# Issuing the routed experts' down weights from ScalarE's DMA queue instead of SyncE's

## Chip, cores and metric

The kernel runs on one core of a Trainium2 chip. The metric is the device time of one execution in microseconds (us), as the median of several runs. Besides TensorE (PE, with its weight loads as PEld), VectorE (DVE), ScalarE (ACT), GpSimd (POOL) and SyncE (SP), the core has 16 DMA engines. They serve several queues: q1 holds what SyncE issues, q10 what ScalarE issues, q0 what GpSimd issues.

## What is computed

One layer of an encoder on 512 tokens of 1024 elements, all in float32: a token mixer (sparse attention beside a gated recurrence), then a mixture of experts. The change is in the second part. Of 64 experts each token uses 8, beside a shared one:

```python
def _moe(u, w_router, router_bias, w_gate, w_up, w_down, ws_gate, ws_up, ws_down):
    scores = jax.nn.sigmoid(t @ w_router)
    ...                                   # best 4 of 8 groups, then the best 8 experts
    gates = jnp.zeros((T, N_EXPERTS)).at[jnp.arange(T)[:, None], top_e].set(w)
    ...
        h = jax.nn.silu(jnp.einsum('td,edf->tef', xb, w_gate)) * jnp.einsum('td,edf->tef', xb, w_up)
        return jnp.einsum('tef,efd->td', h * gb[:, :, None], w_down)
    ...
    shared = (jax.nn.silu(t @ ws_gate) * (t @ ws_up)) @ ws_down
    return routed + shared
```

Gate and up weights of an expert are 1024 x 256, its down weights 256 x 1024: three transfers of 1 MB for each expert, with one row of 8 KB on each of 128 partitions.

## The kernel before

Each engine has its own instruction stream, written out by hand; semaphores order the streams. The mixer fills the first 430 us or so. In the expert part there are `n_steps` steps, here 64, one for each expert. A step takes the rows of the tokens that chose its expert (128 at most), gathers them from DRAM (`u2_rows`) into `xg`, turns them with the PE, multiplies by gate and up weights, applies SiLU and product, turns the result, multiplies by the down weights and stores the 128 result rows (`expert_rows`). The steps run in a hardware loop that is unrolled by `UNROLL = 4`, with the first and the last four written apart. The semaphores count four tiles of the shared expert first, hence the `VIRT = 4` in the counts.

Weights lie in `wx`, in four slots, and step n uses slot n mod 4. Each slot has a semaphore for gate and up (`gu_full`) and one for down (`w_full`).

Products of the down weights and of half of gate and up are made in three passes with a high and a low part: ScalarE writes `wd_hi` and `gu_hi` (L640, L647), VectorE the differences `wd_lo` and `gu_lo` (L914, L919). There is one `wd_hi` buffer, so it can be written for one step when the down product of the step before is through (`y2_done`).

The order in one step, by engine:

- PE (L850): indices of the step after next (`tokens_of`, L804), gate and up product (L756, L761), then the wait for `gathered` and the transposes of the next step's rows (`turn_rows`, L811), then the down product of the step before (L783), then the turn of `hs` (L769).
- GpSimd (L581): waits for the indices of the step after next and gathers its rows (L568).
- VectorE: the two halves of the result row of the step before (`yrow`, L1076, L1077), the next indices (L1046, L1048, L1041), `wd_lo` (L914), `hT_lo` (L933), the product after SiLU (L908), the rows' copies (L924, L927), `gu_lo` (L919).
- ScalarE (L693): after `y2_done` writes `wd_hi` and `hT_hi`, then SiLU of this step (L660), `xT_hi` (L651), and `gu_hi` of the next (L647).
- SyncE (L519): after `gu_done` it loads gate and up of the step four later, after `y2_done` the down weights of the same, and after `y2_left` and `y2_right` it issues the store (L513).

After the loop come the last four steps, and in parallel GpSimd gathers `expert_rows` back for each token, in 32 gathers (L597) that begin when all but the last four stores have landed. The PE adds them up (L877), and the last layer norm follows.

The functions that the change touches, and what they call:

Of the kernel before, what the change touches and what calls it, by code (L numbers as in the profile page):

```python
# [21 lines left out]
NE, ED, NG, TG, EK = 64, 256, 8, 4, 8  # L22
# [12 lines left out]
MAXPASS = NT  # L35
UNROLL = 4
# [30 lines left out]
def build(nc, x, c, w_ada, b_ada, w_in, kv_norm_g, w_uk, w_uv, rel_bias, hgrn_lb, gnorm_g, w_out,  # L67
# [17 lines left out]
    with ExitStack() as ctx:  # L85
# [3 lines left out]
        def sem(name):  # L89
            return ctx.enter_context(nc.semaphore(name))  # L90
# [300 lines left out]
        y2_done = sem("y2_done")  # L391
# [13 lines left out]
        w_full = [sem(f"w_full{i}") for i in range(UNROLL)]  # L405
# [44 lines left out]
        wd_v = w_down[0].rearrange("e (p j) n -> e p (j n)", j=KF)  # L450
# [12 lines left out]
        def flat_weights(s):  # L463
            w = wx[:, s, :, :].rearrange("p a n -> p (a n)")
            return w[:, 0:2048], w[:, 2048:4096], w[:, 4096:6144]

        def steps(eng):

            eng.wait_ge(route_ready, 1)
            more = eng.value_load(nit[0:1, 0:1], min_val=0, max_val=(MAXPASS - 1) * NE)  # L470
            return eng.snap(more + NE)

        def sync_tail(sp):
            sp.wait_ge(rows_used, ROWS)
            for dst, src in zip(flat_weights(SHARED), (ws_gate[0], ws_up[0], ws_down[0])):
                j = KD if src.shape[0] == D else KF
                sp.dma_start(dst, src.rearrange("(p j) n -> p (j n)", j=j)).then_inc(shared_loaded, 16)

            def load(s, e, parts=range(3)):
                for k in parts:  # L480
                    dst, src = flat_weights(s)[k], (wg_v, wu_v, wd_v)[k]
                    sp.dma_start(dst, src[e] if isinstance(e, int) else src[bass.ds(e, 1)].rearrange("o p n -> (o p) n"))\
                        .then_inc(w_full[s] if k == 2 else gu_full[s], 16)

            for t in range(NT):
                if t == NT - 1:
                    sp.wait_ge(wo_done, NT)
                    load(0, 0)
                sp.wait_ge(u2_ready, t + 1)
                sp.dma_start(u2_d[t * P:(t + 1) * P, :], u2[:, t % 2, :]).then_inc(u2_stored[t % 2], 16)  # L490
            sp.wait_ge(x1_ready, NT)
            sp.wait_ge(xg_zero, 2)
            for b_ in range(4):
                sp.dma_start(y_d[T * EK - (b_ + 1) * P:T * EK - b_ * P, :], xg[:, b_ % 2, :]).then_inc(ends_zeroed, 16)
            load(2, 2, (0, 1))
            load(3, 3, (1, 2))
            sp.wait_ge(gu_done, VIRT)
            sp.wait_ge(ends_zeroed, 64)
            for b_ in range(2):
                sp.wait_ge(gathered[b_], 16)  # L500
            load(1, 1, (0, 1))
            load(2, 2, (2,))
            load(3, 3, (0,))
            sp.wait_ge(y2_done, VIRT)
            load(1, 1, (2,))
            n_steps = steps(sp)

            def store(u, row, waits, stored):

                sp.wait_ge(y_stored, stored)  # L510
                sp.wait_ge(y2_left, waits)
                sp.wait_ge(y2_right, waits)
                sp.dma_start(y_d[bass.ds(row, P), :], yb_[:, u % 2, :]).then_inc(y_stored, 16)  # L513

            def first_row(col):
                return sp.value_load(base_i[0:1, bass.ds(col, 1)], min_val=0, max_val=T * EK)

            n16 = sp.snap(n_steps * 16)
            with sp.Fori(0, n_steps - UNROLL, UNROLL) as i:  # L519
                i16 = sp.snap(i * 16)  # L520
                for u in range(UNROLL):
                    done = sp.snap(i + (VIRT + u + 1))
                    stored = sp.snap(i16 + (u + 4) * 16)
                    row = first_row(i + u)
                    e = sp.snap((i + (UNROLL + u)) % NE)

                    sp.wait_ge(gu_done, done)
                    load(u, e, (0, 1))
                    sp.wait_ge(y2_done, done)
                    load(u, e, (2,))  # L530
                    store(u, row, done, stored)
            for u in range(UNROLL):
                done = sp.snap(n_steps + (VIRT + u + 1 - UNROLL))
                row = first_row(n_steps + (u - UNROLL))
                stored = n16 + u * 16

                done = sp.snap(sp.to_reg(done), min_val=1, max_val=1024)
                store(u, row, done, stored)
            sp.dma_start(lnrow[:, 0, :], ln2_g[0:1, :].broadcast_to([P, D])).then_inc(ln_loaded, 16)
            sp.dma_start(lnrow[:, 1, :], ln2_b[0:1, :].broadcast_to([P, D])).then_inc(ln_loaded, 16)  # L540
            for t in range(NT):
                if t < NT - 1:
                    sp.wait_ge(row_out, t + 1)
                else:
                    sp.wait_ge(last_out, 1)
                sp.dma_start(out_t[:, t, :], x1[:, t, :]).then_inc(out_stored, 16)
            sp.wait_ge(out_stored, 16 * NT)
# [90 lines left out]
        def act_tail(act):  # L638
            def weights_high(s):
                act.activation(wd_hi[:], flat_weights(s)[2], ACT.Copy).then_inc(wd_hi_ready, 1)  # L640

            def gate_up_high(s, loaded, used):

                act.wait_ge(gu_full[s], loaded)
                if used is not None:
                    act.wait_ge(gu_done, used)
                act.activation(gu_hi[:], gate_up_weights(s)[:, :, 0:J3, :], ACT.Copy).then_inc(gu_hi_ready, 1)  # L647

            def rows_high(n):
                act.wait_ge(xt2_done, n + 1)  # L650
                act.activation(xT_hi[:], ps[2][:, 0:J3 * P].rearrange("p (j n) -> p j n", n=P), ACT.Copy).then_inc(xt2_act, 1)  # L651
# [4 lines left out]
            def silu_gate(n, u):  # L656
                act.wait_ge(gu_done, n + 1)
                if not isinstance(n, int) or n >= 2:
                    act.wait_ge(ht_done, n - 1)
                act.activation(hs[:, u % 2, :], ps[u % 2][:, 0:ED], ACT.Silu).then_inc(silu_ready, 1)  # L660

            def turned(n, u):
                act.wait_ge(ht_done, n + 1)
                if not isinstance(n, int) or n >= 2:
                    act.wait_ge(y2_done, n - 1)
                act.activation(hT_hi[:, u % 2, :, :], ps[4][:, 0:ED].rearrange("p (j n) -> p j n", n=P),
                               ACT.Copy).then_inc(ht_ready, 1)
# [22 lines left out]
            shared_out(3)  # L690
            n_steps = steps(act)

            def expert(i, u, more=True):  # L693
                first = isinstance(i, int)
                if not first or u >= 1:
                    act.wait_ge(y2_done, i + (VIRT + u - 1))
                    act.wait_ge(w_full[(u - 1) % UNROLL], 4 * i + (16 if u >= 1 else 0))
                    weights_high((u - 1) % UNROLL)
                    turned(i + (VIRT + u - 1), u - 1)
                silu_gate(i + (VIRT + u), u)  # L700
                if more:
                    rows_high(i + (u + 1))
                    gate_up_high((u + 1) % UNROLL, 8 * i + (32 if u < UNROLL - 1 else 64), i + (VIRT + u + 1))

            for u in range(UNROLL):
                expert(0, u)
            with act.Fori(UNROLL, n_steps - UNROLL, UNROLL) as i:
                for u in range(UNROLL):
                    expert(i, u)
            tail = act.snap(act.to_reg(n_steps - UNROLL), min_val=NE - UNROLL, max_val=MAXPASS * NE)  # L710
            for u in range(UNROLL):
                expert(tail, u, u < UNROLL - 1)

            def diagonals(first, end):
                for d in range(first, end):
# [460 lines left out]
        def _(sp):  # L1176
# [50 lines left out]
            load_rows(7)  # L1227

            sync_tail(sp)

        @block.gpsimd
# [30 lines left out]
        def _(act):  # L1262
# [215 lines left out]
            act.wait_ge(u2_ready, NT)  # L1478
            act.activation(wd_hi[:], flat_weights(SHARED)[2], ACT.Copy).then_inc(wd_hi_ready, 1)  # L1479
            act_tail(act)  # L1480

        @block.tensor
# [618 lines left out]
```

## Time and profile before

| | |
|---|---|
| runs | 1210.47, 1210.78, 1211.69 us, median 1210.78 |
| the profiled execution | 1211.71 us, span from first to last instruction 1209.9 us |
| busy over the span | PE 93%, PEld 63%, DVE 77%, ACT 40%, POOL 19% |
| bytes | 335.68 MB, of these q1 293.15 MB, q10 8.53 MB, q0 33.58 MB |
| share of 16 DMA engines | q1 64.3%, q10 2.0%, q0 7.5% |

The span lies 1.8 us below the time of the same execution, and that execution is 0.9 us above the median. The shares are means over the whole kernel. The expert loop, from 500 to 1120 us, is the longest stage, and has to be read in its own windows. Matmuls are pipelined, so a busy PE is not a PE at its peak, but a PE without any idle time is one that waits for nobody.

### The profile page before, as it was taken

Reading aid. Unit: us, or ns where it says so; the run is one execution under the profiler, and the core shown is the slowest. Engines: PE = TensorE matmul, PEld = TensorE weight load, DVE = VectorE, ACT = ScalarE, POOL = GpSimd, SP = SyncE. Lnnn points to the kernel's source line nnn. Section 1 sums busy time; section 2 is a strip of 40 time slices with the busy share of each in tenths; the row PEclk is TensorE's granted clock in tenths of the full one; section 3 lists DMA queues with packets and bytes.
Section 4 is the critical chain, followed back from the end, with each engine's and each line's share of the span. In section 5 each row is a group of like instructions: output and inputs, shape, how many; then the busy total and the mean of one; then the engine's idle time right before and its main releaser. Section 6 shows DMA issues by size and latency. Waiting matters only on the chain.

```text
span 1209.9 us, 14757 instructions
## 1 busy us (share of the span) xinstructions
PE 1131.0 (93%) x4784; PEld 760.1 (63%) x4786; DVE 935.9 (77%) x1388; ACT 481.2 (40%) x619; POOL 229.7 (19%) x119
## 2 busy tenths in 40 slices
PE   2699999997999999999999999999999999999965
PEld 2353446885654477677777777777777777777632
DVE  3578997976443777898888888888888888888857
ACT  0214324336651021444444444444444444444411
POOL 0000000000000000122222222222222222222670
PEclk9799999998999989999999999999999999999988
DMA  9992421109302063799999999999999999999793
GB/s 348 356 398 91 50 32 70 70 3 333 118 1 105 35 271 114 277 357 392 382 387 384 384 383 382 374 385 371 392 382 379 376 381 382 376 393 389 259 406 132
DMA packets 77817, 335.68 MB, mean 277 GB/s; under 512 B 14376, under 2 KB 16296, under 8 KB 52824
## 3 DMA queue, kind: packets, MB, share of 16 engines
q1 hardware_dynamic: 58680, 293.15, 64.3%
q0 software_dynamic: 13824, 33.58, 7.5%
q10 hardware_dynamic: 5280, 8.53, 2.0%
q8 instruction: 19, 0.31, 0.1%
q14 instruction: 14, 0.11, 0.0%
HBM read 309.51 MB, written 42.48 MB: 291 GB/s over the span
## 4 chain that ended last, share of the span: by engine, by line
PE 88%; DVE 4%; DMA 3%; ACT 2%; issue 2%; POOL 1%; ACTq 0%; SPq 0%; DVEq 0%; POOLq 0%
PE ps L756 18%; PE ps L783 15%; PE ps L761 14%; PE ps L1521 8%; PE ps L811 5%; PE ps L1751 5%; PE ps L1529 3%; PE ps L821 2%; PE ps L1592 2%; DMA ring<-in_w_ada 2%; PE ps L877 2%; PE ps L1615 2%; PE ps L1605 2%; PE ps L1721 2%; PE ps L1549 1%
## 5 line engine op out<-in xcount | busy, mean ns | idle before, releaser
L568 POOL DMA_INDIRECT xg<-u_rows,idx x64 | 182.9, 2858 | 496.8 <-DVE idx L1048 496.5
L756 PE MATMUL ps<-wx,xT 128*128 128x512 f32 x512 | 235.4, 602 | 0.1
L919 DVE TENSOR_TENSOR gu_lo<-wx,gu_hi 128x2048 fp32r<-128x2048 f32 x64 | 146.6, 2291 | 56.9 <-ACT gu_hi L647 56.9
L914 DVE TENSOR_TENSOR wd_lo<-wx,wd_hi 128x2048 fp32r<-128x2048 f32 x65 | 148.5, 2284 | 2.8 <-ACT wd_hi L1479 2.2
L756 PEld LDWEIGHTS ps<-wx,xT 128*128 128x128 f32 x512 | 92.1, 190 | 92.0 <-issue 91.8
L660 ACT ACTIVATE hs<-ps 128x256 f32<-128x256 f32 x68 | 26.0, 383 | 302.0 <-PE ps L761 281.3
L640 ACT ACTIVATE wd_hi<-wx 128x2048 fp32r<-128x2048 f32 x64 | 122.4, 1913 | 26.3 <-PE ps L783 26.3
L761 PE MATMUL ps<-gu_hi,xT_hi 128*128 128x512 f32 x256 | 126.3, 493 | 0.5 <-DVE gu_lo L919 0.5
L647 ACT ACTIVATE gu_hi<-wx 128x2048 fp32r<-128x2048 f32 x64 | 122.1, 1908 | 0.0
L783 PE MATMUL ps<-wd_hi,hT_hi 128*128 128x512 f32 x272 | 112.7, 414 | 4.3 <-DVE hT_lo L933 4.3
L783 PE MATMUL ps<-wd_hi,hT_lo 128*128 128x512 f32 x272 | 107.3, 395 | 0.0
L783 PE MATMUL ps<-wd_lo,hT_hi 128*128 128x512 f32 x272 | 106.5, 391 | 0.0
L761 PE MATMUL ps<-gu_hi,xT_lo 128*128 128x512 f32 x256 | 101.2, 395 | 0.0
L761 PE MATMUL ps<-gu_lo,xT_hi 128*128 128x512 f32 x256 | 99.5, 389 | 0.0
L1521 PE MATMUL ps<-uT,ring 128*128 128x512 f32 x208 | 91.0, 600 | 0.0
L1521 PEld LDWEIGHTS ps<-uT,ring 128*128 128x128 f32 x208 | 39.9, 193 | 49.9 <-issue 48.8
L811 PEld LDWEIGHTS ps<-ident,xg 128*128 128x128 f32 x512 | 67.0, 191 | 5.2
L811 PE MATMUL ps<-ident,xg 128*128 128x128 f32 x512 | 67.2, 274 | 0.0
L761 PEld LDWEIGHTS ps<-gu_hi,xT_hi 128*128 128x128 f32 x256 | 48.2, 188 | 24.0 <-issue 16.3
L761 PEld LDWEIGHTS ps<-gu_lo,xT_hi 128*128 128x128 f32 x256 | 48.3, 188 | 23.6 <-issue 15.1
L551 POOL MEMSET tri<- 128x64 f32 x1 | 0.2, 151 | 331.3 <-PE ps L1761 331.3
L783 PEld LDWEIGHTS ps<-wd_hi,hT_hi 128*128 128x128 f32 x272 | 51.5, 189 | 14.0 <-DVE hT_lo L933 4.9
(317 smaller groups left out, 1869.6 us busy)
## 6 DMA issues: line engine op xcount, KB each, us to landing
wx<-in_w_gate SPq DMA_DIRECT2D x64, 1024.0 KB, 7.6
wx<-in_w_up SPq DMA_DIRECT2D x64, 1024.0 KB, 10.7
wx<-in_w_down SPq DMA_DIRECT2D x64, 1024.0 KB, 8.5
expert_rows<-yrow SPq DMA_DIRECT2D x64, 512.0 KB
ring<-in_w_ada SPq DMA_DIRECT2D x7, 2048.0 KB, 19.8
ring<-in_w_in SPq DMA_DIRECT2D x6, 2048.0 KB, 15.9
vg<-in_w_ada SPq DMA_DIRECT2D x2, 2048.0 KB, 13.3
fk<-in_w_ada SPq DMA_DIRECT2D x2, 2048.0 KB, 15.2
```

Of the source, the lines that this page charges most:

```text
L568: pool.indirect_dma_start(out=xg[:, buf, :], out_offset=None, in_=u2_d[:, :], in_offset=bass.IndirectOffsetOnAxis(ap=idx[:, col:col + 1], ...
L640: act.activation(wd_hi[:], flat_weights(s)[2], ACT.Copy).then_inc(wd_hi_ready, 1)
L647: act.activation(gu_hi[:], gate_up_weights(s)[:, :, 0:J3, :], ACT.Copy).then_inc(gu_hi_ready, 1)
L756: pe.matmul(bank, xT_raw[:, j - J3, :], raw[:, :, j, :], start=(j == J3), stop=False)
L761: mm = pe.matmul(bank, a[:, j, :], w[:, :, j, :], start=False, stop=(j == J3 - 1 and k == 2))
L783: mm = pe.matmul(ps[6 + half][:], a[:, u % 2, j, :], w[:, j, half * 512:half * 512 + 512], start=(k == 0), stop=(k == len(passes) - 1))
L811: mm = pe.transpose(ps[2 + k][:, j * P:(j + 1) * P], xg[:, buf, 4 * k + j::KD], ident[:])
L914: dve.tensor_tensor(wd_lo[s][:], w, wd_hi[:].bitcast(F32), ALU.subtract).then_inc(wd_ready, 1)
L919: dve.tensor_tensor(gu_lo[s][:, :, 0:J3, :], gate_up_weights(s)[:, :, 0:J3, :], gu_hi[:].bitcast(F32), ALU.subtract).then_inc(gu_lo_ready, 1)
L1521: mm = pe.matmul(bank[:], ring[:, SLOT[unit], j, col:col + P], uT[:, j, :], start=(j == 0), stop=(j == KD - 1))
L1529: mm = pe.matmul(bank[:, 0:w], uT[:, j, t * P:(t + 1) * P], ring[:, SLOT[unit], j, col:col + w], start=(j == 0), stop=(j == KD - 1))
L1751: mm = pe.matmul(ps[2 * (t % 2) + half][:], src[:, j % 4, t * P:(t + 1) * P], ring[:, SLOT[OUT0 + half], j, :], start=(j == 0), stop=(j == ...
```

## The change

SyncE no longer waits for `y2_done` in the loop and no longer issues the down weights there. ScalarE does: in each step from the third on it stops at `y2_done`, computes the address and issues the load of the down weights of the expert two after its own step, into the slot whose down product has just ended. The condition, the slot, the semaphore and the number of loads are those of before; the loads ahead of the loop stay with SyncE. In the last four steps it issues only in the first two. A bound in `tail` is narrowed for the address computation.

```diff
--- before.py
+++ after.py
@@ -526,8 +526,6 @@
 
                     sp.wait_ge(gu_done, done)
                     load(u, e, (0, 1))
-                    sp.wait_ge(y2_done, done)
-                    load(u, e, (2,))
                     store(u, row, done, stored)
@@ -690,10 +688,17 @@
-            def expert(i, u, more=True):
+            def next_down(i, u):
+                e = i + u + 2 if isinstance(i, int) else act.snap((i + (u + 2)) % NE)
+                src = wd_v[e] if isinstance(e, int) else wd_v[bass.ds(e, 1)].rearrange("o p n -> (o p) n")
+                act.dma_start(flat_weights((u + 2) % UNROLL)[2], src).then_inc(w_full[(u + 2) % UNROLL], 16)
+
+            def expert(i, u, more=True, ending=False):
                 first = isinstance(i, int)
                 if not first or u >= 1:
                     act.wait_ge(y2_done, i + (VIRT + u - 1))
+                    if (not first or u >= 2) and (not ending or u < UNROLL - 2):
+                        next_down(i, u)
                     act.wait_ge(w_full[(u - 1) % UNROLL], 4 * i + (16 if u >= 1 else 0))
                     weights_high((u - 1) % UNROLL)
                     turned(i + (VIRT + u - 1), u - 1)
@@ -707,9 +712,9 @@
-            tail = act.snap(act.to_reg(n_steps - UNROLL), min_val=NE - UNROLL, max_val=MAXPASS * NE)
+            tail = act.snap(act.to_reg(n_steps - UNROLL), min_val=NE - UNROLL, max_val=MAXPASS * NE - UNROLL)
             for u in range(UNROLL):
-                expert(tail, u, u < UNROLL - 1)
+                expert(tail, u, u < UNROLL - 1, True)
```

SyncE, one step inside the loop, before (with what each row waits for; ISA and REGISTER_ALU are register work):

```order
L482 ISA [waits gu_done]
L482 DMA wx<-in_w_gate 128x2048
L482 DMA wx<-in_w_up 128x2048
L482 DMA wx<-in_w_down 128x2048 [waits y2_done]
L510 REGISTER_ALU
L513 ISA [waits y2_right,y2_left,y_stored]
L513 DMA expert_rows<-yrow 128x1024
```

and after:

```order
L482 ISA [waits gu_done]
L482 DMA wx<-in_w_gate 128x2048
L482 DMA wx<-in_w_up 128x2048
L510 REGISTER_ALU
L513 ISA [waits y2_right,y2_left,y_stored]
L513 DMA expert_rows<-yrow 128x1024
```

The down load with its wait is gone, and the rest stands in the same order.

ScalarE, the second of the four steps in the loop, before:

```order
L697 REGISTER_ALU [waits y2_done]
L640 ACTIVATE wd_hi<-wx 128x2048 [waits w_full0]
L666 ACTIVATE hT_hi<-ps 128x256 [waits y2_done,ht_done]
L657 REGISTER_ALU
L660 ACTIVATE hs<-ps 128x256 [waits ht_done,gu_done]
L651 ACTIVATE xT_hi<-ps 128x512 [waits xt2_done]
L647 ACTIVATE gu_hi<-wx 128x2048 [waits gu_done,gu_full2]
```

and after:

```order
L694 ISA [waits y2_done]
L694 DMA wx<-in_w_down 128x2048
L702 REGISTER_ALU
L638 ACTIVATE wd_hi<-wx 128x2048 [waits w_full0]
L664 ACTIVATE hT_hi<-ps 128x256 [waits y2_done,ht_done]
L655 REGISTER_ALU
L658 ACTIVATE hs<-ps 128x256 [waits ht_done,gu_done]
L649 ACTIVATE xT_hi<-ps 128x512 [waits xt2_done]
L645 ACTIVATE gu_hi<-wx 128x2048 [waits gu_done,gu_full3]
```

Register work and the load stand between the wait for `y2_done` and `wd_hi`. The other activations keep their places.

## Rows read from the trace of the kernel before

**Rows 1.** Windows: stretch and length, busy us (instructions) by engine, PEclk, DMA share, GB/s

```profile
core 0: us, PE busy (x) PEld busy (x) DVE busy (x) ACT busy (x) POOL busy (x), PEclk, DMA share, GB/s
800.00:880.00 80.00, 80.00 (x365) 57.70 (x364) 67.47 (x88) 37.79 (x39) 23.69 (x8) 1.00 0.98 384
```

**Rows 2.** Timeline, 801 to 816 us: start, duration, engine (q: its sequencer), line, operation

```profile
801.77 2.94 POOL L568 DMA_INDIRECT xg<-u_rows,idx  x1 [7.33 <-DVE idx L1048]
...
807.85 0.33 SPq L482 DMA_DIRECT2D wx<-in_w_down  x1
807.85 1.91 ACT L640 ACTIVATE wd_hi<-wx 128x2048 fp32r<-128x2048 f32 x1 [0.36 <-PE ps L783]
...
809.67 0.37 ACT L666 ACTIVATE hT_hi<-ps 128x256 fp32r<-128x256 f32 x1
...
811.26 0.35 SPq L513 DMA_DIRECT2D expert_rows<-yrow  x1
...
811.83 2.29 DVE L914 TENSOR_TENSOR wd_lo<-wx,wd_hi 128x2048 fp32r<-128x2048 f32 x1
...
812.04 2.94 POOL L568 DMA_INDIRECT xg<-u_rows,idx  x1 [7.33 <-DVE idx L1048]
...
814.05 1.09 PEld L811 LDWEIGHTS ps<-ident,xg 128*128 128x128 f32 x8
...
814.48 0.38 ACT L660 ACTIVATE hs<-ps 128x256 f32<-128x256 f32 x1 [4.44 <-PE ps L761]
...
815.05 0.19 PEld L783 LDWEIGHTS ps<-wd_hi,hT_hi 128*128 128x128 f32 x1
```

**Rows 3.** DMA issues of the page: out<-in, queue, count, KB each, median us to landing

```profile
wx<-in_w_up SPq DMA_DIRECT2D x64, 1024.0 KB, 10.7
```

**Rows 4.** DMA issues in windows of one gather each; the last number is its landing

```profile
xg<-u_rows,idx POOLq DMA_INDIRECT x1, 10.6
...
xg<-u_rows,idx POOLq DMA_INDIRECT x1, 11.3
...
xg<-u_rows,idx POOLq DMA_INDIRECT x1, 11.4
...
xg<-u_rows,idx POOLq DMA_INDIRECT x1, 11.5
...
xg<-u_rows,idx POOLq DMA_INDIRECT x1, 11.7
...
xg<-u_rows,idx POOLq DMA_INDIRECT x1, 12.1
```

**Rows 5.** Line 568, all gathers of the expert loop

```profile
DMA to landing us min/median/max: 4.5/10.8/12.1
```

**Rows 6.** Timeline, issues by ScalarE: start, duration

```profile
17.44 0.55 ACTq L1266 DMA_DIRECT2D wuv<-in_w_uv  x1
18.01 9.69 ACTq L1266 DMA_DIRECT2D rbias<-in_router_bias  x1
...
278.48 0.38 ACTq L1387 DMA_DIRECT2D big<-bias_by_position  x1
```

**Rows 7.** DMA queues from 24 to 27 us: packets, MB, share of 16 engines

```profile
q1 hardware_dynamic: 260, 1.01, 87.1%
q10 hardware_dynamic: 262, 0.15, 16.7%
```

**Rows 8.** DMA queues from 282.25, 818.00, 822.25 (0.25 us each) and 812 (1 us)

```profile
q10 hardware_dynamic: 16, 0.03, 35.8%
...
q0 software_dynamic: 2, 0.01, 8.0%
...
q0 software_dynamic: 1, 0.00, 0.2%
...
q1 hardware_dynamic: 56, 0.43, 102.5%
```

**Rows 9.** Timeline, the end of the expert loop

```profile
1119.48 42.94 SPq L513 DMA_DIRECT2D expert_rows<-yrow  x5
...
1127.86 1.32 POOL L597 DMA_INDIRECT wx<-expert_rows,slot8i  x1 [5.30 <-DMA expert_rows<-yrow]
```

## The prediction

> **What bounds the kernel now.** I read the windows of the expert loop first. In a stretch of 80 us TensorE is busy for all 80.00 us at a granted clock of 1.00, VectorE for 67.5 and ScalarE for 37.8 us, and the 16 DMA engines for 0.98 of the time [rows 1]. Two things are full at once, TensorE and the DMA engines, and only the timeline tells which one sets the pace. One step lasts 10.27 us (the gathers of two steps start at 801.77 and 812.04), and TensorE has no idle time in it [rows 1, 2]. So TensorE sets the pace, and a change of queues can gain nothing inside the loop. The question is only whose slack it eats. I looked at three.
>
> Weights: each of the four slots is loaded anew as soon as its step is through, and wanted again some three steps, 30 us, later. The slowest of the loads, up, lands in 10.7 us in the median [rows 3]. None is near a wait.
>
> ScalarE: wd_hi starts at 807.85, hT_hi follows, and then ScalarE is idle for 4.44 us. VectorE takes up wd_hi only at 811.83 [rows 2].
>
> Row gathers: GpSimd starts one at 801.77, and the transposes that read its rows start at 814.05 [rows 2], 12.28 us later. The median of the 64 landings is 10.8 us and the longest 12.1 [rows 4, 5]. This is the only tight wait of the loop: 1.5 us in the median, 0.2 us once. It also hangs on how the DMA engines share their time, which is what the change alters. The order of the queues is therefore the argument, not their bytes.
>
> **What the change does, part by part.** It removes from SyncE one wait for y2_done and one issue per step (0.33 us at 807.85 [rows 2]). SyncE then stands at the wait for y2_left, y2_right and y_stored as before. The store still starts at 811.26, when VectorE has written the row, and the next gate and up loads follow it. They keep their start, so this part is worth 0.
>
> It adds to ScalarE one address computation, one issue and an earlier stop of its sequencer at y2_done. ScalarE's issues took 0.38 and 0.55 us where its queue had room [rows 6]. With the register work I take 0.5 us per step. Queued behind are wd_hi, hT_hi and the SiLU of the next step. Now wd_hi ends at about 809.8 (807.85 + 1.91) and would end at 810.3, 1.5 us before VectorE starts line 914 at 811.83. hT_hi would be ready at 810.5, and the 4.44 us of idle time before the SiLU take up the rest [rows 2]. Cost 0; if ScalarE lost over 1.5 us more, wd_lo would be late, and behind it the down product at 815.05.
>
> Bounding the issue itself: the longest one of ScalarE took 9.69 us [rows 6]. That was the seventh transfer in a row in its queue. Here each down load is alone in its queue and lands before the next is issued, so I take the short end.
>
> It moves 1 MB per step from SyncE's queue (q1) to ScalarE's (q10). The bytes and the total backlog of the DMA engines stay. What changes is whose turn it is. Where q1 and q10 both have work, they send packet for packet: 260 against 262 from 24 to 27 us [rows 7]. A gather (q0) that now trades turns with q1 alone would have two others between its packets, for as long as q10 is active.
>
> When is q10 active? A ScalarE issue at 278.48, while q1 was full, shows no q10 packet in the quarter of a microsecond from 282.00 and its first 16 in the one from 282.25: 3.8 us [rows 6, 8]. The gather's own instruction (812.04, 2.94 us long) ends at 814.98 and its first two packets stand in 818.00 to 818.25, 3.1 us later [rows 2, 8]. Counted from the gather's start, y2_done comes at 6.1 us (807.85 against 801.77) and ScalarE would issue at 6.2. So q10's packets begin at 9.3 to 10.0, and I take 9.7, between the two. The gather's packets run from 6.1 us to 0.3 us before it lands: the one that lands after 10.6 has its last packet in 822.25 to 822.50, at 10.2 to 10.4 [rows 4, 8]. **So the overlap is the last 0.6 us of a median gather, and up to 2.1 us of the slowest.** After that q10 has the next 5 us (8 packets on each engine, each beside one of q1) and is empty before the next gather's first packet.
>
> The price of a turn: in 812 to 813 us q1 alone sent 56 packets with 0.43 MB, in 102.5% of 16 engine-microseconds [rows 8]. That is about 52 packets of 8 KB at 0.31 us. A round of the gather now costs 0.31 us plus its own packet. The gather's packets are 4 KB rows (half of 0.31, some 0.16 us) or almost nothing. One q10 packet more therefore stretches it by 0.66 to 0.97 of its remaining time; I take 0.85. With landing L a gather would land at L + 0.85 (L - 0.3 - 9.7), and TensorE would wait for 1.85 L - 20.8 us where that is positive, from L = 11.24 on.
>
> Of the 28 landings that the trace tells between 540 and 1110 us (it tells every other one), three are 11.4, two 11.5, and one each 11.3, 11.7 and 12.1; the other 20 are 11.2 or less [rows 4] (a row that comes again stands once). The waits are 0.1 + 3 x 0.3 + 2 x 0.5 + 0.85 + 1.6 = 4.45 us, and doubled for the untold half 8.9 us. A wait gives something back: in the step in which TensorE waits, y2_done and the down load come later too, and the next gather has more time. Where the next gather would be late as well (8 in 28) this removes its wait; 8.9 less 8/28 of it is 6.4 us. Bounds: a start at 9.3 and a factor of 0.97 give waits from 10.96 on, some 21 us before and 12 to 15 after the same reduction; a start at 10.0 and 0.66 give 2.7 us before and 2 after.
>
> **The tail.** Behind the last down load stands the store of step 59, issued at 1119.48. GpSimd then waits 5.30 us, until 1127.86, for that store, before it begins the 32 gathers of expert rows [rows 9]. With the down load out of its queue the store could land earlier by at most that load's 8 packets per engine, 8 x 0.31 = 2.5 us. Against it: the engine that is last has the same packets to send in either order, and taking turns brings store and load to an end together. I take -0.9 us, between 0 and -2.5 and nearer to 0.
>
> **The sum.** 6.4 - 0.9 = +5.5 us. The profiled execution took 1211.71 us, of which 1209.9 are its span, and the median of the runs is 1210.78. The difference goes on the median: 1216.3 us, +0.45%.
>
> **What a page says.** The rows show the queues taking turns by packets [rows 7]. The Trainium skill, "DMA: Bandwidth & Descriptors", section "Queues, rings and completion order", says that each DMA engine goes round its queues packet by packet. The same page, section "Issuing engines are not separate DMA queues", says that issuing from several engines saves only the issuing sequencer's time. By the second rule the sum would be 0, by the first a third queue costs a waiting gather turns. Both can hold, since the bytes per second stay and one transfer's share falls; no run so far shows three queues at work.
>
> **Rivals.**
> No effect (0.36): the q10 packets start at 10.2 us or later, or the last engine's gather packets are already through. For it: the median gather has only 0.6 us of overlap, and 20 of 28 stay under the break-even of 11.24. Against it: eight do not. It gives 1210.8 less some of the tail, 1209.5 to 1212. This is also what the rule of the second section above comes to.
> Faster by the tail (0.13): the store of step 59 lands 2.5 us earlier, GpSimd's 32 gathers start as much earlier, and all behind them too, since TensorE has waits for just these gathers. It decides if the last engine sends the store before the load's last packets. 1210.8 - 2.5 = 1208.3.
> More than the overlap (0.05): ScalarE's issue blocks as in the 9.69 us row, or a third queue also puts off the gather's first packet. 1 us in each of 56 steps less 0.2 to 1.5 us of slack gives 1230 and more.
> The overlap as computed: 0.46, of which the lowest tenth lies within 0.2%.
>
> **How the numbers follow.** 0.2%, 2.4 us, is about what a measurement of this kernel can tell from no change. Slower by more: 0.41 + 0.05 = 0.46. Within: 0.36 plus 0.05 of the overlap's low end = 0.41. Faster: 0.13. The likeliest case gives 1216.3, on its own 1212.5 to 1226. The range takes in the tail's gain and the overlap's upper bound, and leaves out the fourth case: 1208.4 to 1226.
>
> **What would show it.** Each step right: TensorE idle before line 811, only in steps whose gather lands after 12.28 us; q10 packets first seen 9.3 to 10 us after a gather's start; the longest landings grow and the short ones do not; down loads land at 7 to 9 us, gate and up loads as before; ScalarE's idle before the SiLU falls from 4.44 to about 3.9 us. It is wrong if no gather lands after 12.28 us (then the second case), if VectorE waits for wd_hi inside the loop, or if GpSimd's 5.30 us shrinks to under 4 us and the loop keeps 10.27 us (then the third).

## The result and the profile after

The changed kernel takes 1222.80 us in the median of 13 runs (1214.31 to 1231.53). The kernel before, run beside it, takes 1213.37 (1210.37 to 1219.34, 13 runs). The ratio is 1.0075 [1.0055, 1.0096]: slower by about 9 us. The profiled execution took 1224.19 us, of which 1222.4 are its span, against 1211.71 and 1209.9 before: the span is 12.5 us longer. No ratio here counts one execution of 1488.74 us at a granted clock of 0.745, of the kernel under "The load behind the gather", which ran in a slower state of the core.

Parts 4 to 6 of the page of the kernel after (shares of the chain of waits; costliest groups with busy, mean ns and idle time before; DMA issues with their landing):

```profile
PE 70%; DMA 15%; DVE 5%; issue 4%; ACT 3%; POOL 2%; ACTq 0%; SPq 0%; POOLq 0%; DVEq 0%
...
L816 PEld LDWEIGHTS ps<-ident,xg 128*128 128x128 f32 x512 | 65.9, 192 | 18.7 <-DMA xg<-u_rows,idx 14.7
...
wx<-in_w_up SPq DMA_DIRECT2D x64, 1024.0 KB, 12.7
```

Line 4 of the page before:

```profile
PE 88%; DVE 4%; DMA 3%; ACT 2%; issue 2%; POOL 1%; ACTq 0%; SPq 0%; DVEq 0%; POOLq 0%
```

TensorE held 88% of the chain and now holds 70%; DMA went from 3% to 15%. The line that got a wait is 816, the row transposes (line 811 before): TensorE's weight loads wait 14.7 us in sum in front of them for the gathered rows. The up load lands 2.0 us later than in [rows 3], which nobody notices, since it has 30 us.

A window of 550 us, nearly the whole expert loop, in the columns of [rows 1], before and then after:

```profile
560.00:1110.00 550.00, 550.00 (x2461) 392.17 (x2460) 465.89 (x590) 266.37 (x268) 156.91 (x54) 1.00 0.99 383
```

```profile
560.00:1110.00 550.00, 542.74 (x2415) 383.59 (x2413) 456.84 (x578) 261.88 (x263) 153.73 (x52) 1.00 0.98 375
```

TensorE was busy for all of the 550 us. Now it stands idle for 7.3 of them, at the same granted clock of 1.00. It is waiting, not slower. These 7.3 us are less than the loop lost (below). PE's own waits for the gathered rows are shorter than those of its weight loads, 0.66 us against 1.08 in the step shown below and 8.5 against 14.7 in sum, and the 14.7 come nearer to the loss.

The time is located by one line of the trace, that of the 64 row gathers: the first and the last start bound the loop. Before:

```profile
L568 POOL DMA_INDIRECT xg<-u_rows,idx x64: 988/2939/3042, 463.6 to 1120.3; - x64
```

After, with those that waited for the rows (us, times) and the landings:

```profile
L566 POOL DMA_INDIRECT xg<-u_rows,idx x64: 985/2935/3042, 462.4 to 1131.4; - x64
...
  PEld ps L816: 14.7, 15
...
DMA to landing us min/median/max: 4.2/11.6/14.5
```

From first to last gather it was 656.7 us and is 669.0. The difference of the two spans, 12.5 us, splits into -1.2 ahead of the loop, **+12.3 in it** and +1.4 behind it. Landings were 4.5/10.8/12.1 [rows 5]; the median is 0.8 and the longest 2.4 us later, and the shortest is not. (The trace of the kernel before tells the landing of every other gather, so the median in [rows 5] is one of 32 and not of 64; this one tells all 64. The packets of q0 are there for every gather: counted over the 54 gathers 7 to 60, the last packet ends 10.6 us after the gather's start in the median before, and 11.3 us after the change. It ends later than 11.98 us, 0.3 us ahead of the 12.28, in none before and in 15 after, as many as there are waits.)

One such step on the timeline of the kernel after (815 to 830 us):

```profile
816.67 2.94 POOL L566 DMA_INDIRECT xg<-u_rows,idx  x1 [8.09 <-DVE idx L1053]
...
822.92 0.34 ACTq L694 DMA_DIRECT2D wx<-in_w_down  x1
...
823.40 1.91 ACT L638 ACTIVATE wd_hi<-wx 128x2048 fp32r<-128x2048 f32 x1 [1.01 <-PE ps L788]
...
826.81 2.29 DVE L919 TENSOR_TENSOR wd_lo<-wx,wd_hi 128x2048 fp32r<-128x2048 f32 x1
...
829.36 0.38 ACT L658 ACTIVATE hs<-ps 128x256 f32<-128x256 f32 x1 [3.78 <-PE ps L766]
...
829.98 0.97 PEld L816 LDWEIGHTS ps<-ident,xg 128*128 128x128 f32 x8 [1.08 <-DMA xg<-u_rows,idx]
```

Its gather and its landing in the list of DMA issues, and the first quarter of a microsecond (824.50 to 824.75) with packets of q10, ScalarE's queue:

```profile
xg<-u_rows,idx POOLq DMA_INDIRECT x1, 13.3
```

```profile
q10 hardware_dynamic: 2, 0.02, 75.5%
```

The gather starts at 816.67 and lands 13.3 us later, 1.0 us past the 12.28 us that it has, and TensorE waits 1.08 us. ScalarE issued the down load 6.25 us after the gather's start. Its packets begin 1.6 to 1.8 us after that, 7.8 to 8.1 us after the gather's start, when the gather has five microseconds to go. This step is a typical one: over the 54 the first q10 packet comes 8.3 us after the gather's start in the median, between 7.5 and 9.6. ScalarE itself loses nothing: wd_hi starts 1.01 us after its release instead of 0.36 [rows 2], ends at 825.31, and VectorE takes it up at 826.81, 1.5 us later.

### The profile page after: what moved, and what is told of

It reads as the page before. It is cut to its first block, busy times and chain, and to the rows that moved or that the text cites. A ratio compares the mean times of both kernels' runs of the same rounds, so it can differ in the third digit from the quotient of the medians.

```text
span 1222.4 us, 14787 instructions
## 1 busy us (share of the span) xinstructions
PE 1135.9 (93%) x4786; PEld 759.9 (62%) x4786; DVE 935.9 (77%) x1388; ACT 481.1 (39%) x619; POOL 230.5 (19%) x119
## 4 chain that ended last, share of the span: by engine, by line
PE 70%; DMA 15%; DVE 5%; issue 4%; ACT 3%; POOL 2%; ACTq 0%; SPq 0%; POOLq 0%; DVEq 0%
DMA xg<-u_rows,idx 12%; PE ps L761 12%; PE ps L788 10%; PE ps L766 9%; PE ps L1526 7%; PE ps L1756 4%; PE ps L816 4%; PE ps L1534 3%; PE ps L826 2%; PE ps L1597 2%; DMA ring<-in_w_ada 2%; PE ps L882 2%; PE ps L1620 2%; PE ps L1610 2%; PE ps L1726 2%
## 5 line engine op out<-in xcount | busy, mean ns | idle before, releaser
L924 DVE TENSOR_TENSOR gu_lo<-wx,gu_hi 128x2048 fp32r<-128x2048 f32 x64 | 146.6, 2291 | 56.9 <-ACT gu_hi L645 56.9
L816 PEld LDWEIGHTS ps<-ident,xg 128*128 128x128 f32 x512 | 65.9, 192 | 18.7 <-DMA xg<-u_rows,idx 14.7
## 6 DMA issues: line engine op xcount, KB each, us to landing
wx<-in_w_up SPq DMA_DIRECT2D x64, 1024.0 KB, 12.7
vg<-in_w_ada SPq DMA_DIRECT2D x2, 2048.0 KB, 13.1
```

The costliest lines, as they stand in the source:

```text
L816: mm = pe.transpose(ps[2 + k][:, j * P:(j + 1) * P], xg[:, buf, 4 * k + j::KD], ident[:])
L924: dve.tensor_tensor(gu_lo[s][:, :, 0:J3, :], gate_up_weights(s)[:, :, 0:J3, :], gu_hi[:].bitcast(F32), ALU.subtract).then_inc(gu_lo_ready, 1)
```

## The experiments

**The theory of turns:** a third active queue stretches the gather that it overlaps, and the price is the length of its turns in the gather's last microseconds. Rivals: ScalarE's stop and address work delay wd_hi; the bytes or the backlog matter and not the order; the difference is one of run to run. In the expectations a loop of "595.9 us" is counted from the sixth gather; the loop here is always counted from the first, which makes it 656.7 for the same kernel. Differences are the same either way.

**Once more, both.** The kernel before and the kernel after, unchanged, in a later comparison.

> The kernel before once more, for a second trace. If its spread of 1208.8 to 1222.8 us comes from outside the expert loop, the stretch from the fourth to the last row gather is 595.9 us again, whatever the total is. If it comes from late gathers in some executions, that stretch is longer where the total is above 1211 us, and TensorE waits before the row transposes.

> The changed kernel once more, for a second trace and a ratio beside the other two. Turn theory: waits of 8 to 20 us before the row transposes, the loop's stretch 604 to 616 us against 595.9, median landing 11.3 to 12, ratio 1.005 to 1.010. If the first trace was a chance: a loop near 596 us and a ratio below 1.003.

The kernel before: 1218.56 us in one profiled execution. The kernel after: 1.0092 [1.0065, 1.0119]. Line of the gathers, before again and then after again:

```profile
L568 POOL DMA_INDIRECT xg<-u_rows,idx x64: 985/2939/3043, 470.3 to 1127.0; - x64
...
  PEld ps L811: 0.2, 1
```

```profile
L566 POOL DMA_INDIRECT xg<-u_rows,idx x64: 987/2941/3044, 468.8 to 1131.0; - x64
...
  PEld ps L816: 6.7, 8
...
DMA to landing us min/median/max: 5.2/10.9/13.9
```

The loop of the kernel before is 656.7 us again, to a tenth, with one wait of 0.2. That of the kernel after is 662.2: +5.5, where the other trace had +12.3. The sum of the waits is a matter of how many gathers land beyond 12.28 us, 8 here and 15 there. The median landing is 10.9 us here, only 0.1 later than in [rows 5], but that is again every other gather; by the last packets of the 54 it is 10.9 against 10.3 in the kernel before again, 0.6 us later. The kernel before again took 6.8 us more than the first trace of it, nearly all ahead of the loop (first gather at 470.3, not 463.6). The first 120 us, first trace of before and then the second:

```profile
0.00:120.00 120.00, 87.16 (x284) 47.23 (x285) 74.88 (x112) 25.20 (x51) 3.77 (x16) 0.90 0.82 300
```

```profile
0.00:120.00 120.00, 87.56 (x269) 47.90 (x270) 69.55 (x94) 22.71 (x47) 3.77 (x16) 0.83 0.81 299
```

The granted clock was 0.90 and 0.83 (the third number from the end), and 269 products instead of 284 were through. It is so in all thirteen traces: in the four with a clock of 0.82 or 0.83 there the first gather starts at 468.5 to 470.9 us, in the nine with 0.90 to 0.93 at 460.6 to 466.3. This goes a long way to explain why single times of one kernel spread over 9 us. I therefore set the length of the loop, which is free of it, beside each ratio.

**ScalarE's share alone.** The kernel before, and ScalarE does all that the change gives it, but loads 8 bytes per partition into a buffer that nobody reads; SyncE still loads the down weights.

```diff
+            def next_down(i, u):
+                e = i + u + 2 if isinstance(i, int) else act.snap((i + (u + 2)) % NE)
...
+                act.dma_start(small_dst[:], src[:, 0:2]).then_inc(small_sem, 16)
```

> The kernel before, with its down loads left in SyncE's queue; ScalarE issues in the same place a load of 8 bytes per partition that nobody reads, with the same address work. Turn theory (a gather lands late because packets of 8 KB of a third queue come between its own): a turn of 8 bytes costs nothing, so gathers land after 10.8 us in the median as before, TensorE does not wait before its row transposes, ratio to before 0.998 to 1.002. Rival, ScalarE's time (the stop at y2_done, the register work and the issue cost the loop): the ratio is that of the changed kernel, 1.0075. Rival, bandwidth (q1 and q10 together move less per second): ratio 1.000 too, since hardly any bytes are on q10.

1.0009 [0.9986, 1.0031]. Its gathers, then its ScalarE on the timeline:

```profile
L570 POOL DMA_INDIRECT xg<-u_rows,idx x64: 984/2939/3043, 463.6 to 1121.0; - x64
...
  PEld ps L823: 1.0, 2
```

```profile
809.18 1.91 ACT L642 ACTIVATE wd_hi<-wx 128x2048 fp32r<-128x2048 f32 x1 [0.98 <-PE ps L795]
```

The same delay of wd_hi as in the kernel after (0.98 against 1.01 us), and a loop of 657.4, +0.7. ScalarE's work is not the cause. (This kernel waits besides for its own small load of the step before, which has long landed. Its q10 packets come later than those of the kernel after, 9.7 us after the gather's start in the median, so that it tests ScalarE's work and not the place of the packets.)

**The same load, later on ScalarE.** The kernel after with `next_down` moved behind `turned`, and in another run behind `silu_gate`:

```diff
-                    if (not first or u >= 2) and (not ending or u < UNROLL - 2):
-                        next_down(i, u)
                     act.wait_ge(w_full[(u - 1) % UNROLL], 4 * i + (16 if u >= 1 else 0))
                     weights_high((u - 1) % UNROLL)
                     turned(i + (VIRT + u - 1), u - 1)
+                    if (not first or u >= 2) and (not ending or u < UNROLL - 2):
+                        next_down(i, u)
                 silu_gate(i + (VIRT + u), u)
```

> The changed kernel, with ScalarE's issue of the down load moved behind wd_hi and hT_hi of the same step, some 2.3 us later; bytes and queues as in the changed kernel. Turn theory: q10's first packets fall 9.5 us or more after the gather's start instead of 7.5 to 9.5, when most gathers are through, and they are gone before the next gather's first packet at 16.4; waits before the row transposes fall from 14.7 us to under 3 us, ratio to before 1.000 to 1.002. ScalarE's time: the issue still stands in the stream, with less behind it, so 1.003 to 1.0075. Bandwidth: nothing changes, 1.0075.

1.0044 [1.0020, 1.0069]. Its timeline:

```profile
803.17 1.91 ACT L638 ACTIVATE wd_hi<-wx 128x2048 fp32r<-128x2048 f32 x1 [0.36 <-PE ps L788]
803.57 0.34 ACTq L694 DMA_DIRECT2D wx<-in_w_down  x1
```

The edit did not do what I meant: the issue stands behind two activations in the code, but ScalarE's sequencer issued it 0.40 us after the first of them had begun, while that one ran on. It came 6.48 us after the gather's start (797.09), 0.2 us later than in the kernel after, and the loop, from 466.3 to 1126.4, is 660.1 (+3.4). This run tells little of the place.

> The changed kernel, with the issue moved further, behind the SiLU of the step, some 13 us after the gather's start. Turn theory: q10's packets now run from about 15 to 20 us and meet the next gather's packets (16.4 to 20.8) from the first on; landings of 12.5 us and more in the median, TensorE waits in most steps, 0.5 to 1 us in the mean step, ratio 1.02 to 1.04. ScalarE's time: the issue stands in idle time and costs nothing, ratio 1.000. Bandwidth: 1.0075.

1.0422 [1.0391, 1.0452], 1263.11 us. The start of its loop's line and the waits:

```profile
L566 POOL DMA_INDIRECT xg<-u_rows,idx x64: 988/2939/3043, 460.6 to 1168.6; - x64
...
  PEld ps L816: 52.3, 34
```

Three of its gathers and the issue on the timeline:

```profile
790.61 2.94 POOL L566 DMA_INDIRECT xg<-u_rows,idx  x1 [7.98 <-DVE idx L1053]
802.61 3.02 POOL L566 DMA_INDIRECT xg<-u_rows,idx  x1 [9.07 <-DVE idx L1053]
812.87 2.94 POOL L566 DMA_INDIRECT xg<-u_rows,idx  x1 [7.23 <-DVE idx L1053]
```

```profile
805.19 0.34 ACTq L694 DMA_DIRECT2D wx<-in_w_down  x1
```

The same bytes in the same queue, issued 2.6 us after the start of a gather, so that they overlap all of it (the first q10 packet comes 6.4 us after the gather's start in the median, its own first at 6.5): the loop is 708.0, +51.3, with 52.3 us of waits. A step of 12.00 us is followed by one of 10.26 here, since a wait in one step gives the next gather more time. The place of the load in relation to the gather decides, and the rival that only bytes count is out.

This trace also shows what three queues do when all have work. From 7 to 9 us after a gather's start, first in the kernel before (819.04 to 821.04) and then here (819.87 to 821.87):

```profile
q1 hardware_dynamic: 76, 0.52, 80.1%
q0 software_dynamic: 96, 0.18, 25.4%
```

```profile
q10 hardware_dynamic: 51, 0.42, 49.2%
q1 hardware_dynamic: 46, 0.37, 43.5%
q0 software_dynamic: 45, 0.08, 10.6%
```

The three send about as many packets each, and the gather's rate is halved. Over all 54 gathers it is 45 packets per microsecond before and 24 here in this stretch, with 23 of q1 and 25 of q10 beside them.

**Half of it.** SyncE loads half of each down weight after `y2_done` as before, ScalarE the other half.

```diff
+                    sp.wait_ge(y2_done, done)
+                    sp.dma_start(flat_weights(u)[2][:, 0:1024], wd_v[bass.ds(e, 1)].rearrange("o p n -> (o p) n")[:, 0:1024])\
+                        .then_inc(w_full[u], 16)
                     store(u, row, done, stored)
...
-                act.dma_start(flat_weights((u + 2) % UNROLL)[2], src).then_inc(w_full[(u + 2) % UNROLL], 16)
+                act.dma_start(flat_weights((u + 2) % UNROLL)[2][:, 1024:2048], src[:, 1024:2048]).then_inc(w_full[(u + 2) % UNROLL], 16)
```

> The changed kernel with half of each down load (columns 0 to 1023 of each partition's row) back in SyncE's queue at its old place, the other half issued by ScalarE where the change puts it: q10's packets are of 4 KB, half as long, as many as before. Turn theory: each turn costs half, waits before the row transposes of 2 to 7 us instead of 14.7, gathers land after about 11.2 us in the median, ratio 1.001 to 1.004. ScalarE's time: issue as in the changed kernel, 1.0075. Bandwidth: between, 1.003 to 1.0075.

1.0013 [0.9991, 1.0034]. Its gathers:

```profile
L569 POOL DMA_INDIRECT xg<-u_rows,idx x64: 987/2937/3042, 463.5 to 1123.5; - x64
...
  PEld ps L819: 4.3, 7
```

Loop 660.0, +3.3, less than either trace of the kernel after. Shorter turns of ScalarE's queue cost less, as the theory asks, but so would halved bytes in it. And a third thing differs, which I had not meant: q10's first packet comes 9.7 us after the gather's start in the median (9.1 to 10.1) and not 8.3, though ScalarE issues at the same 6.26 us. So this run alone says little about the length of a turn. The next runs keep all bytes in q10, and there it starts at 8.3 to 8.4 us, as in the kernel after.

**Turns of half the length, all bytes.** Every weight load is cut into two of half a row's width, so the packets are 4 KB; queues, bytes, engines and places stay. Once on the kernel after, once on the kernel before, and once with only ScalarE's down load cut.

```diff
-                act.dma_start(flat_weights((u + 2) % UNROLL)[2], src).then_inc(w_full[(u + 2) % UNROLL], 16)
+                for a in (0, 1024):
+                    act.dma_start(flat_weights((u + 2) % UNROLL)[2][:, a:a + 1024], src[:, a:a + 1024]).then_inc(w_full[(u + 2) % UNROLL], 16)
```

SyncE's loads are cut in the same manner, and the counts of the semaphores doubled.

> The changed kernel with every weight load of the routed experts, on both queues, issued as two loads of 4 KB per partition instead of one of 8 KB; bytes, places and queues stay. Turn theory: a turn lasts 0.16 us instead of 0.31, on q1 as on q10, so even with three queues a gather's round costs no more than it did before with two; gathers land after 10.0 to 11.0 us in the median, waits before the row transposes under 2 us, ratio to before 0.996 to 1.002. Bandwidth theory (two queues move less per second): smaller packets do not help, 1.0075 or more.

> The changed kernel with all weight loads in rows of 4 KB once more, with more rounds, to tell whether it beats the kernel before. Its loop cannot be shorter than TensorE's work, so 595.9 us as before; what is left is the tail and the spread of the early stage. I expect the same time: ratio 0.998 to 1.001, no waits before the row transposes.

> The kernel before with its weight loads cut into rows of 4 KB as well, all in SyncE's queue. Turn theory: gathers land earlier than before, 9.0 to 10.0 us in the median, nobody waits for one, and what single executions of the kernel before lose above 1210 us goes with it: ratio 0.995 to 0.999, with less spread. If the spread of the kernel before comes from elsewhere: 1.000, the same spread. If SyncE's two to three more issues per step or the smaller packets cost rate: above 1.001.

> The changed kernel with only the down loads cut, into two loads of 4 KB per partition, both issued by ScalarE at the place of the change; gate and up stay at 8 KB. All bytes are on q10 as in the changed kernel, but a turn of q10 lasts half as long. Turn theory: what counts is the length of a turn during the overlap, not the bytes, so nearly as with half of the load: waits of 3 to 8 us, ratio 1.001 to 1.004. If the bytes on q10 count: 1.0075.

The kernel after, cut: 0.9983 [0.9957, 1.0009], and on another chip 1.0002 [0.9980, 1.0024]. The landings of its gathers in the first run:

```profile
DMA to landing us min/median/max: 4.3/9.6/11.0
```

Nothing waited for them; the loop, from 468.5 to 1125.2, is 656.7, as before the change. The other trace has 656.7 too. With ScalarE's queue and all its bytes in place, halving the turns took away the whole loss. The kernel before, cut, is 1.0020 [0.9997, 1.0042] and has a loop of 656.7 as well. Its gathers land at 4.6/9.9/10.7 us, earlier than uncut (10.8 in [rows 5]).

So the cut helps the gathers of both kernels, by 0.9 us in the median before the change and by 1.3 and 2.0 after it, and buys nothing where they were in time. With the down load alone cut: 1.0003 [0.9979, 1.0026], with these waits for the gathered rows:

```profile
  PEld ps L817: 3.5, 8
```

The loop, from 462.0 to 1120.9, is 658.9, +2.2. This is the run that changes nothing but the length of q10's packets, and by its ratio most of the loss is gone. Some waits are left; q1's packets are still 8 KB, and that this is why is not shown.

**The load behind the gather.** The kernel with the load behind `turned`, and ahead of it a wait for `ht_ready`, so that ScalarE really issues later.

```diff
                     turned(i + (VIRT + u - 1), u - 1)
+                    if (not first or u >= 2) and (not ending or u < UNROLL - 2):
+                        act.wait_ge(ht_ready, i + (VIRT + u))
+                        next_down(i, u)
```

> The changed kernel with the issue moved behind hT_hi and with a wait of ScalarE's sequencer for it (ht_ready), so that it really comes some 2 us later; in the run that only moved the instruction the issue came 0.2 us later, since the sequencer does not stand behind its own activations. Turn theory: issue at 8.3 us after the gather's start, first q10 packets at 9.5 to 11, waits 1 to 4 us in sum, ratio 1.000 to 1.003. ScalarE's time: the sequencer stops longer, 1.0075 or more. Bandwidth: 1.0075.

1.0042 [1.0019, 1.0066]. The landings are 5.2/10.6/11.7 and the loop is 656.7 again, with one wait of 0.8 us:

```profile
L566 POOL DMA_INDIRECT xg<-u_rows,idx x64: 986/2939/3043, 465.9 to 1122.6; - x64
...
  PEld ps L817: 0.8, 1
```

The loss in the loop is gone with 8 KB packets too, once the load comes behind the gather (here it is issued 8.5 us after the gather's start, and its first packet comes 11.7 us after it in the median). The kernel is still slower, since another transfer pays. The end of its loop on the timeline:

```profile
1120.92 0.68 DVE L1083 TENSOR_TENSOR yrow<-ps,vg 128x512 f32<-128x512 f32 x1
...
1122.64 2.28 POOL L566 DMA_INDIRECT xg<-u_rows,idx  x1 [7.29 <-DVE idx L1054]
1125.37 9.96 SPq L513 DMA_DIRECT2D expert_rows<-yrow  x2
...
1135.71 0.99 POOL L595 DMA_INDIRECT wx<-expert_rows,slot8i  x1 [10.78 <-DMA expert_rows<-yrow]
```

VectorE has written the row at 1121.60, and SyncE issues the store only at 1125.37: a store is issued only when the one before has landed (`y_stored`), and the down load now lies beside the stores. GpSimd waits 10.78 us for the last one, where it waited 5.30 [rows 9] or, in the second trace, 3.96 us, and begins the expert rows 13.1 us after the last gather instead of 7.6 or 6.2. From the last gather to the end of the span it is 92.4 us, before 89.6 and 89.8: +2.6 to 2.8. That is less than the ratio's middle (5 us) and within its interval; whether there is more is open.

## Why the prediction came out as it did

The direction and the place of the loss were right, and the time lies in the range. The size was forecast as +5.5 us (0.45%); it is 0.75% and 0.92% in two comparisons, some 9 to 11 us. Two terms that make up the size were wrong, in opposite directions, so that it came out near by luck.

- **SyncE, and the slack of the weights.** Right at nothing. I had said that the up load would land as before; it lands 2.0 us later, but has far more slack than that.
- **ScalarE, 0.5 us per step, hidden.** Right. The delay is 0.65 us (1.01 less 0.36), the idle time before the SiLU went from 4.44 [rows 2] to 3.78 where I had said 3.9, and the load nobody reads, with the same work, gave a loop of +0.7.
- **q10's start, 9.3 to 10.0 us after the gather's.** Wrong, and the first of the mis-sized terms. I took the delay from issue to first packet from one issue under a full q1 and from the gather, 3.1 to 3.8 us [rows 6, 8]. In the kernel after it is 1.8 us in the median of 54 steps (1.9 in its second trace), and q10 starts at 8.3 us. The overlap of a median gather, whose last packet ended at 10.6, was so some 2.3 us and not 0.6. My 9.7 is what the two kernels show in which SyncE still issues its own load 0.2 us ahead of ScalarE's: 3.4 us from issue to first packet and a start at 9.7, both with the load nobody reads and with half of it. The change takes that issue of SyncE away. That it is the cause of the shorter delay is not shown, only that the two go together.
- **The price of a turn, 0.66 to 0.97 of the overlap.** Wrong the other way. By my formula a start at 8.3 takes a median landing of 10.8 to 10.8 + 0.85 x (10.8 - 0.3 - 8.3) = 12.7, and many steps would wait. By the last packets it went up by 0.7 us in one pair of traces and 0.6 in the other, which is a price of about 0.3. The longest landing went from 12.1 to 14.5 and 13.9, some 0.5 to 0.7 of its overlap of 3.5 us (the gathers of two traces are not paired, so these are rough).

  The turns themselves are as forecast. With all three queues at work, under the load behind `silu_gate`, they sent packet for packet and the gather's rate was halved. What I had wrong is the sentence that a gather would have two others between its packets for as long as q10 is active. It supposes that q1 goes on having work, and since the change it mostly has not. The queues of the kernel after in the first 2.5 us in which q10 is active beside a gather (824.5 to 827.0):

```profile
q10 hardware_dynamic: 46, 0.38, 52.8%
q1 hardware_dynamic: 43, 0.27, 26.1%
q0 software_dynamic: 71, 0.16, 17.7%
```

  The like numbers of q10 and q1 here come of the window: from 8.3 to 10.3 us after the start, over 54 gathers, q1 sends 24 packets per microsecond where it sent 46 before the change, and q10 19. At q10's first packet only 47 of the 256 weight packets that q1 has in a step are still to be sent (50 in the second trace), about three for each of the 16 DMA engines. So q10 in the main takes turns that q1's own down load had before. The gather sends 31 and 32 packets per microsecond in this stretch in the two traces after, and 32 and 31 before: on average it loses nothing. What is late is the end of it. Of its 144 packets 0.2 and 0.4 were sent more than 11 us after its start before the change, and 2.3 and 1.9 are since. A gather has landed when its last packet has. That these few sit on engines that still have work of all three queues would fit, but the trace does not tell a packet's engine, and which gathers are hit stays open.

  So the overlap of the median gather was put at a quarter of what it is and its price at nearly three times, and 6.4 us of waits came out where two traces have 14.7 and 6.7.
- **A wait gives the next gather more time.** Shown plainly by the load behind `silu_gate`, with its long and short steps.
- **The tail, -0.9.** Wrong; there is no gain. The end of the loop in the kernel after (the row of VectorE is of L924, the difference `gu_lo`):

```profile
1131.42 2.28 POOL L566 DMA_INDIRECT xg<-u_rows,idx  x1 [7.29 <-DVE idx L1053]
...
1137.17 2.28 DVE L924 TENSOR_TENSOR gu_lo<-wx,gu_hi 128x2048 fp32r<-128x2048 f32 x1
1137.36 2.95 POOL L595 DMA_INDIRECT wx<-expert_rows,slot8i  x1 [3.66 <-DMA expert_rows<-yrow]
...
1140.62 3.10 POOL L595 DMA_INDIRECT wx<-expert_rows,slot8i  x1 [0.30 <-issue]
```

  and the first two of the 32 gathers in the kernel before, the second of its first trace and the first of its second trace:

```profile
1129.48 3.09 POOL L597 DMA_INDIRECT wx<-expert_rows,slot8i  x1 [0.30 <-issue]
```

```profile
1133.26 2.66 POOL L597 DMA_INDIRECT wx<-expert_rows,slot8i  x1 [3.96 <-DMA expert_rows<-yrow]
```

  GpSimd waits 3.66 us here and 3.87 in the second trace after, and 5.30 [rows 9] and 3.96 in the two before. So it is not clear that the store lands earlier at all. Nor would it help: a first gather that starts 1.6 us sooner takes 2.95 us instead of 1.32 [rows 9]. Both end 8.9 us after the last row gather's start, 0.9 us after VectorE has ended `gu_lo`, and the second starts 9.20 us after it in both kernels (1140.62 less 1131.42, 1129.48 less 1120.28). The gain ends there. What is then left is +1.4 us in one trace and +0.3 to 0.5 in the other; its cause is open.

The rivals: no effect is out, with both intervals above 1.005. Faster by the tail fell at the step just named. That ScalarE's issue blocks is out: it took 0.33 to 0.35 us in each of the 60. That a third queue puts off the gather's first packet is out too: it comes 6.2 us after the gather's start before and 6.3 after, in the median. The rule of the Trainium skill that I had weighed, "DMA: Bandwidth & Descriptors", section "Issuing engines are not separate DMA queues", would have made the sum 0. That moving a transfer to another engine's queue brings no bandwidth, this trace bears out (375 GB/s in the loop after the change, 383 before). That it saves only issue time and does nothing else, it does not: the gathers lost 0.7 and 0.6 us in the median, and with another place of the same load the kernel lost 4.2%. The measurement decides.

No version tried beats the kernel before: the best, cut into 4 KB packets, is at 0.9983 and 1.0002. TensorE is busy for 652.9 of the loop's 656.7 us, and for all of the 550 shown above, so no order of queues gets far below it.

## What to carry to other kernels

Before a transfer is moved to another engine's queue, look for the latency-critical one among those it will now lie beside, and compare its landing with the time it has: an added queue takes turns, and what decides is when in that transfer's life it does, whether the other queues still have work then, and how long its packets are. A price per turn holds only while all queues are full (24 instead of 45 packets per microsecond here); where the moved load takes turns that it had before in its old queue, only the last few packets come late. Halving the packets took away the whole loss at no cost in rate (383 GB/s in the loop), which is a simpler remedy here than a new order. And a wait that one moves out of the way may lead to the next transfer in line, as the stores here.

## What the runs showed of the hardware that I had not expected

- ScalarE's sequencer doesn't hold a DMA issue behind activations that stand ahead of it in the code and have not ended: it was issued 0.40 us after the start of one of 1.91 us. To issue later takes a semaphore.
- From ScalarE's issue to its first packet it was 1.8 and 1.9 us in the median in the two traces of the kernel after, with q1 at work, and 3.4 us in both kernels in which SyncE issues a load 0.2 us before it; it was 3.8 us in the issue of [rows 6, 8]. What makes the difference is open.
- With three queues full, each sends about as many packets (51, 46 and 45 in 2 us), whatever their length.
- GpSimd's instruction for a row gather ends 0.86 to 0.87 us after VectorE has ended the `wd_lo` beside it, in each of the 54 of every trace. It takes 2.94 us in the median; a gather of expert rows that meets no such difference takes 0.99 us (at 1135.71 above).
- Packets of 4 KB instead of 8 KB landed the gathers at 9.6 to 9.9 us in the median instead of 10.8, with the loop's rate unchanged.
- The loop takes 656.7 us to a tenth in six traces of four kernels, while the stretch ahead of it differs by up to 7.6 us in these six, and by 10.3 in all thirteen, with the granted clock of its first 120 us.
